# The first weight sum of each group of products: an accumulating transfer from GpSimd's queue in place of an addition on VectorE

## The reference

```python
hm = _rms(x, norm_mlp) @ w_up                 # (tokens, 2048) @ (2048, 8192)
x = x + jnp.square(jax.nn.relu(hm)) @ w_down  # (tokens, 8192) @ (8192, 2048)
```

## Time and profile before

| | us |
|---|---|
| median of 3 runs | 2752.1 (2750.05 to 2752.74) |
| the profiled execution, its own time | 2752.23 |
| its span in the profile | 2750.6 |
| TensorE matmul busy | 2629.5 (96% of the span) |
| VectorE busy | 1772.8 (64%) |
| ScalarE busy | 991.2 (36%) |
| GpSimd busy | 127.7 (5%) |
| hardware queue, share of the 16 DMA engines' span | 32.5% |
| software queue, the same | 17.7% |

### The profile page before, as it was taken

One profiled execution on the slowest core, in us unless ns is written; L12 is line 12 of the kernel. 1 busy time (PEld: TensorE's weight loads), 2 busy tenths in 40 slices (PEclk: granted clock), 3 DMA queues, 4 the chain that ended last, 5 costly groups with the idle time before them and its releaser, 6 DMA issues.

```text
span 2750.6 us, 48550 instructions
## 1 busy us (share of the span) xinstructions
PE 2629.5 (96%) x20400; PEld 2565.1 (93%) x20400; DVE 1772.8 (64%) x2107; ACT 991.2 (36%) x1222; POOL 127.7 (5%) x194
## 2 busy tenths in 40 slices
PE   8999999999999999997599999999979999999995
PEld 7989999999999979887599999999969999999995
DVE  7647433343552242435888888888857888888887
ACT  6532211111321121222455555655533333333332
POOL 1100000000000010000000000000011000000000
PEclk9999999999999999998799999999989999999998
DMA  7763222222233454532266666566677666567643
GB/s 270 228 216 95 95 84 87 90 84 92 86 109 125 149 199 161 186 121 79 71 228 215 211 220 231 208 217 218 233 269 272 229 223 224 197 216 240 220 132 104
DMA packets 136872, 476.84 MB, mean 173 GB/s; under 512 B 12128, under 2 KB 18400, under 8 KB 128512
## 3 DMA queue, kind: packets, MB, share of 16 engines
q1 hardware_dynamic: 105728, 293.08, 32.5%
q0 software_dynamic: 30976, 181.32, 17.7%
HBM read 398.23 MB, written 76.12 MB: 172 GB/s over the span
## 4 chain that ended last, share of the span: by engine, by line
PE 90%; DMA 4%; DVE 4%; issue 1%; ACT 1%; SPq 0%; POOL 0%; DVEq 0%; POOLq 0%; ACTq 0%
PE psum_main L1432 38%; PE psum_main L1792 26%; PE psum_side L1792 19%; PE psum_main L1539 3%; DMA hidden<-hidden_kept 1%; DMA cache_ring_a<-cache_v 1%; DMA unit_raw<-weights 1%; PE psum_main L1716 1%; DVE tokens L1238 1%; PE psum_side L1612 1%; DVE unit_low L1214 0%; DVE residual L1232 0%; ACT unit_high L741 0%; PE psum_main L1647 0%; DVE residual L1419 0%
## 5 line engine op out<-in xcount | busy, mean ns | idle before, releaser
L741 ACT ACTIVATE unit_high<-unit_raw 128x1024 fp32r<-128x1024 f32 x384 | 402.3, 1056 | 572.5 <-DVE unit_raw L1292 146.9
L1432 PE MATMUL psum_main<-inner_a,unit_high 128*128 128x272 f32 x3584 | 599.9, 289 | 0.0
L1214 DVE TENSOR_TENSOR unit_low<-unit_raw,unit_high 128x1024 fp32r<-128x1024 f32 x384 | 468.7, 1221 | 124.8 <-ACT unit_high L741 123.9
L571 ACT ACTIVATE unit_high<-unit_raw 128x1024 fp32r<-128x1024 f32 x226 | 239.3, 1060 | 771.2 <-PE psum_main L1432 718.2
L1432 PEld LDWEIGHTS psum_main<-inner_a,unit_high 128*128 128x128 f32 x3584 | 507.2, 188 | 3.5 <-issue 3.4
L1792 PE MATMUL psum_main<-tokens,unit_high 128*128 128x272 f32 x2048 | 392.4, 290 | 44.8 <-DVE unit_low L1214 23.1
L841 DVE TENSOR_TENSOR unit_low<-unit_raw,unit_high 128x1024 fp32r<-128x1024 f32 x226 | 276.3, 1225 | 239.6 <-ACT unit_high L571 236.9
L1792 PE MATMUL psum_main<-hidden,unit_high 128*128 128x272 f32 x2048 | 391.0, 289 | 21.5 <-DVE residual L1337 21.1
L1432 PE MATMUL psum_main<-inner_a,unit_low 128*128 128x272 f32 x1792 | 369.9, 287 | 0.0
L1792 PEld LDWEIGHTS psum_main<-tokens,unit_high 128*128 128x128 f32 x2048 | 325.4, 191 | 45.4 <-issue 45.4
L1792 PEld LDWEIGHTS psum_main<-hidden,unit_high 128*128 128x128 f32 x2048 | 323.8, 190 | 22.6 <-DVE residual L1337 21.9
(11 more groups left out here) (189 smaller groups left out, 3304.2 us busy)
## 6 DMA issues: line engine op xcount, KB each, us to landing
unit_raw<-weights SPq DMA_DIRECT2D x482, 512.0 KB, 4.2
hidden_kept<-hidden_staged POOLq DMA_DIRECT2D x32, 1904.0 KB, 6.9
hidden<-hidden_kept POOLq DMA_DIRECT2D x56, 1088.0 KB, 7.1
unit_sum<-weights SPq DMA_DIRECT2D x64, 512.0 KB, 3.7
cache_ring_a<-cache_v POOLq DMA_DIRECT2D x16, 1024.0 KB, 6.6
cache_ring_t<-cache_k POOLq DMA_DIRECT2D x8, 1024.0 KB, 7.9
cache_ring_a<-cache_k POOLq DMA_DIRECT2D x8, 1024.0 KB, 6.7
residual<-x_t POOLq DMA_DIRECT2D x8, 544.0 KB, 5.6
```

Source lines behind the costliest of these rows:

```text
L571: act.activation(WHI[:, s, :], RAW[:, s, :], ACT.Copy).then_inc(high_ready, 1)
L741: act.activation(WHI[:, slot, :], raw, ACT.Copy).then_inc(mlp_high, 1)
L1214: dve.tensor_tensor(WLO[:, slot, :], raw, WHI[:, slot, :].bitcast(F32), ALU.subtract) \
L1432: ins = pe.matmul(out, weights_at(w), moving, start=first and n == 0, stop=last and n == len(passes) - 1)
```

## The change

sum_1 is no longer done on DVE. POOL issues a transfer that reads w21 from DRAM a second time and adds it into SUMW, where SP has put w22. Its semaphore is `first_sum`. Product 3's `high` and sum_2 wait for it. The remaining three sums are renumbered in `mlp_sum`, and sum_3 waits for its two blocks instead of for sum_1.

```diff
-SUM_OF = {2: 3, 3: 1, 4: 2, 5: 4}
+SUM_OF = {2: 2, 4: 1, 5: 3}
...
+        first_sum = sem("first_sum")
...
-                    sp.wait_ge(mlp_sum, 4 * q)
+                    sp.wait_ge(mlp_sum, 3 * q)
...
+            def add_third_block(q):
+                pool.wait_ge(mlp_raw[4], 16 * (q + 1))
+                pool.dma_start(into(q, SUMW[:, :]), blocks(q)[2], accum_op=ALU.add).then_inc(first_sum, 16)
+            add_third_block(0)
+            add_third_block(1)
             for q in range(QUADS - 2):
+                add_third_block(q + 2)
                 store_hidden(q)
+            add_third_block(QUADS)
             pool.wait_ge(hid_stored, 16 * HK)
...
                     pool.wait_ge(mlp_used, PRODUCTS * quad + 3 * (i % 2) + 1)
                     load_hidden(c, i)
+                    if i % 2 == 0:
+                        add_third_block(quad + 1)
+            for q in range(2 * QUADS - 3, 2 * QUADS):
+                add_third_block(q)
...
-                if i in SUM_OF:
-                    act.wait_ge(mlp_sum, 4 * q + SUM_OF[i])
+                if i == 3:
+                    act.wait_ge(first_sum, 16 * (q + 1))
+                elif i in SUM_OF:
+                    act.wait_ge(mlp_sum, 3 * q + SUM_OF[i])
...
-            def sum_1(q):
-                dve.wait_ge(mlp_raw[2], 16 * (q + 1))
-                dve.wait_ge(mlp_raw[4], 16 * (q + 1))
-                dve.tensor_tensor(SUMW[:, :], SUMW[:, :], RAW[:, 2, :], ALU.add).then_inc(mlp_sum, 1)
...
             def sum_2(q):
-                dve.wait_ge(mlp_sum, 4 * q + 2)
+                dve.wait_ge(first_sum, 16 * (q + 1))
+                dve.wait_ge(mlp_sum, 3 * q + 1)
...
-            sum_1(0)
             sum_3(0)
...
-                if q + 1 < 2 * QUADS:
-                    sum_1(q + 1)
```

More of the change, by code:

```diff
@@ L338, in count, with blocks, into @@
             return u[0] * RING + (u[1] + 1)
+        def blocks(q):
+            if q < QUADS:
+                c, j = q // HK, q % HK
+                u = MLP + c * 4 * CH + 2 * j
+                return weights[u], weights[u + 1], weights[u + 2 * HK], weights[u + 2 * HK + 1]
+            c, g = (q - QUADS) // 4, q % 4
+            u = MLP + c * 4 * CH + 2 * CH + 4 * g
+            first = weights[u:u + 2].rearrange("u p n -> p u n")
+            second = weights[u + 2:u + 4].rearrange("u p n -> p u n")
+            return tuple(w[:, :, n:n + 512] for w in (first, second) for n in (0, 512))
+        def into(q, tile):
+            return tile if q < QUADS else tile.rearrange("p (u n) -> p u n", u=2)
         @block.sync
@@ L360, in _ @@
                 load(MLP // RING, s)
[L362 to L375, removed]
             for q in range(2 * QUADS):
@@ L1273, in _, with sum_3 @@
                 low_tokens(6, g, 13 + g)
-            def sum_1(q):
+            def sum_3(q):
                 dve.wait_ge(mlp_raw[2], 16 * (q + 1))
-                dve.wait_ge(mlp_raw[4], 16 * (q + 1))
-                dve.tensor_tensor(SUMW[:, :], SUMW[:, :], RAW[:, 2, :], ALU.add).then_inc(mlp_sum, 1)
-            def sum_3(q):
                 dve.wait_ge(mlp_raw[0], 16 * (q + 1))
-                dve.wait_ge(mlp_sum, 4 * q + 1)
                 dve.tensor_tensor(RAW[:, 2, :], RAW[:, 2, :], RAW[:, 0, :], ALU.add).then_inc(mlp_sum, 1)
             def sum_2(q):
-                dve.wait_ge(mlp_sum, 4 * q + 2)
+                dve.wait_ge(first_sum, 16 * (q + 1))
+                dve.wait_ge(mlp_sum, 3 * q + 1)
                 dve.tensor_tensor(RAW[:, 0, :], RAW[:, 0, :], SUMW[:, :], ALU.add).then_inc(mlp_sum, 1)
             def sum_4(q):
-                dve.wait_ge(mlp_sum, 4 * q + 3)
+                dve.wait_ge(mlp_sum, 3 * q + 2)
                 dve.tensor_tensor(RAW[:, 1, :], RAW[:, 1, :], RAW[:, 0, :], ALU.add).then_inc(mlp_sum, 1)
```

## The result

| | before | after |
|---|---|---|
| time, median | 2752.4 us (4 runs, 2750.1 to 2757.2) | 2784.6 us (4 runs, 2784.5 to 2793.3) |
| profiled execution: its span | 2750.6 us | 2782.8 us |
| ratio of the times | | 1.0124, interval 1.0103 to 1.0144 |

The changed kernel is 1.2% slower, 32.2 us by the medians and by the spans. The forecast was 2774.5 with a range of 2764 to 2795. Of the 10 us that it missed, most lie in two terms: the transfer of group 32 (+3.6) and the steady down stage (+4.1).

What follows compares the result with a forecast made beforehand. TensorE, fully busy in steady work, was taken as the bound, with VectorE and DMA having time to spare. -1.2 + 4.5 + 19.7 + 2.3 - 3.0 = +22.3 on 2752.2 gave 2774.5 us, range 2764 to 2795.

Steps and rivals of the forecast that it cites:

- only three places matter: Gain or loss only at the MLP's start, at the change of stage, or where the new transfer comes too late.
- The start: First summed product of the MLP: sum_1(0) leaves VectorE's unbroken row, so product 2 starts 1.2 us sooner; -1.2.
- Group 32's transfer: Change of stage: its wait for SUMW on POOL delays the loads of hidden values; +4.5, bounds 0 and 6.7.
- Group 33's transfer: Change of stage: issued behind the last residual piece, it holds up sum_2(33) and TensorE; +19.7, bounds 15.7 and 32.1.
- T: Time at which group 33's addition lands, taken as 2081 us; bounds 2077.0 and 2093.4.
- The cold product: After the stall at group 33 TensorE returns cold, its 24 matmuls taking 5.27 us instead of 3.0; +2.3.
- Given back: After group 33's stall, most of TensorE's later waits of 2.8 and 1.1 us go; -3.0, bounds 0 and -3.9.
- Steady down work: Down stage in steady work: the new transfers land in time and cost TensorE nothing; 0.
- A transfer of 5.6 to 7.1 us fits both: Steady up and down stages: the transfer lands within the free 11.7 and 10.4 us, 3.3 us spare in the tighter.
- the first rival: Steady work: each transfer is too late; 2805 if 1 us late in the down stage, 2852 or more if severe; chance 0.20.
- The second rival: Group 33: the stall is nearly absorbed in a stretch limited by DMA; +1.7, 2753.9, no change; chance 0.04.
- the third: Change of stage: VectorE paces TensorE there, so fewer additions make it faster by 6.3, 2745.9; chance 0.02.

Runs made afterwards that it cites:

- experiment 5: Changed kernel with accumulating transfers in groups 0 to 31 only; groups 32 to 63 have the addition on VectorE back: 2751.0 us, 0.9994.
- Experiment 7: Kernel before, with sum_1, sum_3 and sum_2 of group 0 alone made by accumulating transfers: 2747.9 us, 0.9987.
- experiment 6: Kernel before, with GpSimd waiting for SUMW of group 32 ahead of the first load of hidden values, no transfer added: 2757.9 us, 1.0021.
- Experiment 1: Changed kernel with group 33's transfer issued early, ahead of the last hidden store and the last residual piece: 2778.8 us, 1.0095.
- experiment 4: Changed kernel with its 64 transfers as plain copies of w21 over SUMW, without the addition: 2776.3 us, one time.
- experiments 3: Changed kernel with group 32's transfer behind the first load of hidden values and group 33's transfer issued early: 2770.4 us, 1.0061.
- experiment 9: Changed kernel with transfers 32 and 33 moved as in experiments 3, and 34 ahead of the second and third load of chunk 1: 2768.3 us, 1.0059.
- experiment 8: Changed kernel with the first sum of groups 32 to 35 on VectorE again, the other 60 by transfer: 2762.2 us, 1.0049.

## Why the prediction came out right

**TensorE sets the time, and only three places matter: right.** The up stage took 32 transfers at no cost (experiment 5, and 610.5 us from group 2 to group 31 in every trace), with VectorE's busy share falling from 84 to 79 of 100 and the DMA share rising from 0.61 to 0.73.

**The start, -1.2: right.** Product 2 of group 0 began 31.9 us after SUMW's issue in place of 33.2, and group 32 came 1.6 us sooner in the change and 1.9 in experiment 5. Experiment 7 shows that the reason holds for the sums that stand beside it.

**Group 32's transfer, +4.5 with bounds of 0 and 6.7: the direction right, the size too small.** Measured +8.1. I had counted the wait in GpSimd's list and a first load that shares the engines with the weights. The wait alone is 2.8 (experiment 6). The third load went out at 2023.77, 7.8 us later than before and not 5.3. The first had gone out at 2003.71 and took 12.1 us, not the 11.1 that I gave it, beside the new transfer, whose traffic the sum left out; with a plain copy beside it it took 9.3. And between the landing of the second load and the issue of the third stood 1.5 us in place of 0.5, for a reason that the traces don't tell. Both were missing from the upper bound, which was therefore too low.

**Group 33's transfer, +19.7: right, in place and size.** Measured 20.7, behind the last store, as worked out; T, when the addition lands, was 2081 in the old trace, which is 2089.3 with the 8.3 us that had been lost by then, and sum_2(33) began at 2090.3. Experiment 1 takes the wait away by the place in the list, and experiment 4 leaves it in with a plain copy. What the prediction didn't see is that it is not one transfer: with number 33 moved, number 34 holds VectorE up by 10.8 us.

**The cold product, +2.3: right** (2.4). **Given back, -3.0: -4.4,** near the bound of -3.9, which had not counted a third wait of 0.5.

**Steady down work, 0: wrong, +4.1 by the waits and +6.2 by the starts of the products.** The step that failed is "A transfer of 5.6 to 7.1 us fits both, with 3.3 us to spare in the tighter stage". In the down stage it lands in 7.8 to 10.2 us. The prediction had named this sign itself: it was to be wrong if steady windows show TensorE under 100, and 2300 to 2400 us has 96.7. The slack itself was well read: 8.8 us to sum_2 and 10.4 to TensorE. With these landing times sum_2 waits for the transfer in 11 groups (9.8 us in all, 2.0 at most), and TensorE hardly notices. A second effect was missing altogether. The transfer takes 3.0 us of all 16 engines, and loads that run beside it are late: ScalarE waited for raw weights 15 times from 2150 to 2700, 9 times before; it is 14 to 21 times in the six kernels with additions in that stage and 9 to 12 in the four without transfers. With the cheaper copy VectorE doesn't wait there for the transfer at all, and ScalarE waits 7 times. This is the mild end of the first rival, whose price I had set by landing times over 10.4 us alone. Its severe forms, 2852 and more, did not come.

**The second rival (the stall is absorbed) and the third (faster): out.** The stall cost most of its length: of the 20.7 us, 4.4 came back by the waits and 5.8 by the starts of the products; only experiment 7, which has the start alone, is faster.

The signs of the terms held, but for the steady down stage, and so did the mechanism of the largest. That the time lies in the range is in part luck: two terms came out above all that the sum allowed them (8.1 against 6.7, and the steady stage against 0), and what made room for them was the upper bound of 32.1 at group 33, where 20.7 came. The sum of the errors, +3.6 at group 32, +1.0 at group 33, +4.1 in the down stage, -1.4 given back, -0.4 and +0.1 in the small terms, is +7.0. The other 3 us are 1.8 of a later start of the MLP, in code that is the same, and 1.1 that the waits don't show; by the starts of the products, the steady down stage is 2.1 larger, the part given back 1.4, and 0.6 lies behind the MLP.

## What to carry to other kernels

A small urgent transfer that is put into a queue beside large ones takes the place in line of the list that issues it: look, for each of them, at what the issuing engine waits for ahead of it and how many bytes stand before it in the queue, and go on to the next transfer when one is mended. Work taken off an engine that has time to spare gains nothing in steady state, while the DMA engines pay for it, here with 1.9 times the time of a copy; use it only where that engine's row of work sets the end, as at the start here. When bounding the cost of a transfer, count the time that it takes from its neighbours beside its own landing.

## What the runs showed of the hardware

- An accumulating transfer of 512 KB from DRAM to the on-chip memory took 3.00 us of all 16 DMA engines, a plain one in the same place 1.58, and landed in 8.3 against 5.9 us (medians). The profile counts the same bytes for both and 64 packets more for the addition, so that neither GB/s nor MB show the cost; the busy share does.
- GpSimd's queue made an addition of 512 KB wait for what stood ahead of it: 22.3 and 22.8 us to landing behind 1904 KB and three loads of 1088 KB (experiments 3 and 1), 17.0 behind 1904 KB and one such load (experiment 9). In the changed kernel the same two took 12.1. There VectorE stood still meanwhile, and I think that fewer weight loads beside it are the reason; no run separates this.
- In experiment 8 the granted clock fell to 0.66 in a window of 10 us in which TensorE had 2.6 us without work. 42 matmuls fewer ran in it than before, 5.2 us of work, so that the short wait cost twice its length. Waits of 3.3 to 3.8 us in experiments 5 to 7 were followed by the same fall, the two of 1.4 us in the kernel before were not (1.00).
- Raw weight loads of 512 KB in SyncE's queue took longer beside the transfers in GpSimd's: 24 of 103 took over 8 us with the additions (2150 to 2700 us), 18 of 104 with plain copies, 3 of 104 in the kernel before and 6 of 104 in experiment 5, which has none in that stage.
